# Turning the next expert's gathered rows between the up product and the last expert's down product, with result banks by parity

## What is computed

```python
    combine = jnp.zeros((n, N_EXPERTS), jnp.float32).at[rows[:, None], eid].add(w)
    y = jnp.zeros((n, D_MODEL), jnp.float32)
    for e in range(N_EXPERTS):
        h = jax.nn.silu(xt @ w_gate[e]) * (xt @ w_up[e])
        y = y + combine[:, e:e + 1] * (h @ w_down[e]).astype(jnp.float32)
```

## Time and profile before

| | us |
|---|---|
| median of 3 runs | 955.26 |
| lowest, highest | 954.05, 960.38 |
| the profiled execution | 958.91 |
| span of its profile | 957.2 |
| TensorE busy, products and transposes | 800.9 |
| VectorE, ScalarE, GpSimd busy | 253.7, 172.9, 127.2 |

### The profile page before, as it was taken

One profiled execution on the slowest core, in us unless ns is written; L12 is line 12 of the kernel. 1 busy time (PEld: TensorE's weight loads), 2 busy tenths in 40 slices (PEclk: granted clock), 3 DMA queues, 4 the chain that ended last, 5 costly groups with the idle time before them and its releaser, 6 DMA issues.

```text
span 957.2 us, 14486 instructions
## 1 busy us (share of the span) xinstructions
PE 800.9 (84%) x5352; PEld 576.7 (60%) x5352; DVE 253.7 (27%) x652; ACT 172.9 (18%) x430; POOL 127.2 (13%) x195
## 2 busy tenths in 40 slices
PE   4999999989426856994998579999999999999970
PEld 3474856559305524563454577777777777777740
DVE  2880132020334574663123501110000000000003
ACT  2110111211202612654122110000000000010003
POOL 2103020221431320000000110111111111111010
PEclk9999997989757877997999579999999999999995
DMA  9925341422872843007512537988888888888425
GB/s 375 348 98 169 130 137 49 120 81 80 281 235 61 272 131 140 38 2 302 212 45 74 223 133 265 309 300 307 308 303 303 305 313 301 304 299 314 137 30 205
DMA packets 50201, 192.34 MB, mean 201 GB/s; under 512 B 8129, under 2 KB 25954, under 8 KB 43490
## 3 DMA queue, kind: packets, MB, share of 16 engines
q1 hardware_dynamic: 37346, 155.40, 44.6%
q0 software_dynamic: 12800, 36.22, 13.9%
HBM read 178.20 MB, written 17.33 MB: 204 GB/s over the span
## 4 chain that ended last, share of the span: by engine, by line
PE 72%; issue 9%; DMA 5%; DVE 5%; POOLq 4%; POOL 2%; ACT 2%; SPq 0%; DVEq 0%; ACTq 0%
PE pb L465 66%; POOLq L302 2%; POOL ring L303 2%; PE pb L877 2%; DMA x_rows<-kvn,qbd 1%; PE pb L721 1%; DVE vnr L1673 1%; DMA cst<-in_consts_dram 1%; DMA ring<-in_sel_pages_dram 1%; POOLq L303 1%; PE pb L647 1%; DMA tabs<-in_g_dram 1%; DVE xr L1350 1%; PE pb L790 1%; DVE xr L1391 1%
## 5 line engine op out<-in xcount | busy, mean ns | idle before, releaser
L465 PE MATMUL pb<-vnr,ring 128*128 128x128 f32 x2048 | 235.1, 277 | 12.6 <-DVE vnr L1673 12.6
L465 PEld LDWEIGHTS pb<-vnr,ring 128*128 128x128 f32 x2048 | 232.0, 193 | 16.6 <-DVE vnr L1673 16.6
L465 PE MATMUL pb<-ring,xr 128*32 128x128 f32 (+3 forms) x896 | 143.2, 370 | 0.0
L465 PE MATMUL pb<-ring,qT 128*128 128x512 f32 x256 | 112.6, 592 | 0.9 <-DVE kvn L1688 0.9
L465 PEld LDWEIGHTS pb<-ring,xr 128*32 128x32 f32 (+1 forms) x896 | 74.6, 138 | 62.4 <-issue 59.5
L465 PEld LDWEIGHTS pb<-ring,qT 128*128 128x128 f32 x256 | 47.4, 190 | 55.3 <-issue 55.3
L1678 DVE TENSOR_TENSOR qT<-qT,pb 128x512 f32<-128x512 f32 x16 | 11.0, 688 | 236.5 <-PE pb L465 236.5
L1801 POOL DMA_INDIRECT x_rows<-kvn,qbd x16 | 25.3, 1579 | 330.5 <-DVE kvn L1688 330.5
L465 PE MATMUL pb<-ring 128*128 128x128 f32 (+1 forms) x512 | 63.5, 289 | 4.5 <-DMA ring<-in_cmp_pages_dram 3.3
L465 PEld LDWEIGHTS pb<-ring 128*128 128x128 f32 x512 | 62.7, 201 | 5.1 <-issue 3.7
L465 PE MATMUL pb<-ring,work 128*128 128x512 f32 (+2 forms) x256 | 62.8, 473 | 0.0
(11 more groups left out here) (296 smaller groups left out, 666.1 us busy)
## 6 DMA issues: line engine op xcount, KB each, us to landing
ring<-in_w_gate_dram SPq DMA_DIRECT2D x16, 2048.0 KB, 9.1
ring<-in_w_up_dram SPq DMA_DIRECT2D x16, 2048.0 KB, 8.6
ring<-in_w_down_dram SPq DMA_DIRECT2D x16, 2048.0 KB, 10.1
ring<-in_cmp_pages_dram SPq DMA_DIRECT2D x65, 128.0 KB, 2.8
ring<-in_w_in_dram SPq DMA_DIRECT2D x4, 2048.0 KB, 9.9
ring<-in_sel_pages_dram SPq DMA_DIRECT2D x64, 128.0 KB, 2.9
ring<-in_sel_pages_dram POOLq DMA_DIRECT2D x64, 128.0 KB, 3.0
ring<-in_cmp_pages_dram POOLq DMA_DIRECT2D x63, 128.0 KB, 2.9
```

Source lines behind the costliest of these rows:

```text
L465: return nc.tensor.matmul(out, lhsT, rhs, start=start, stop=stop)
```

## The change

The transposes become a unit of their own, `rows_turned`, which TensorE calls through the new argument `ahead` of `expert_units`. T of n+1 then stands behind U of n and ahead of D of n-1; T0 and T1 stand directly ahead of their G, as before. The result banks of D go by parity: pb4 and pb5 for even experts, pb6 and pb7 for odd ones. The semaphore `y_out` is split in two, one for each scaling engine, and D of n waits for the scalings of n-2. ScalarE now does silu n, copy n+1, scale n-1; VectorE copy n+1, multiply n, scale n-1. TensorE waits for the flag ahead of the experts, since the flag's value was formed in pb7. The part for further passes gets waits of its own and does not run here. SP's order of loads and POOL's order of gathers and adds are as before.

```diff
@@ -269,23 +269,32 @@
             if not isinstance(value, int) or value > 0:
                 eng.wait_ge(sem(name), value)
 
-        def expert_units(b, first, eng, last):
-
-
+        def expert_units(b, first, eng, last, ahead=None):
 
             def unit(e, half, par):
 
                 return e, b * E + e, par, b * (E // 2) + half
 
+            def turn(*u):
+
+                if ahead is not None:
+                    ahead(*unit(*u))
+
+            turn(0, 0, 0)
             first(*unit(0, 0, 0))
+            turn(1, 0, 1)
             first(*unit(1, 0, 1))
+            turn(2, 1, 0)
             last(*unit(0, 0, 0))
             first(*unit(2, 1, 0))
+            turn(3, 1, 1)
             last(*unit(1, 0, 1))
             with eng.Fori(1, E // 2 - 1) as m:
                 first(*unit(2 * m + 1, m, 1))
+                turn(2 * m + 2, m + 1, 0)
                 last(*unit(2 * m, m, 0))
                 first(*unit(2 * m + 2, m + 1, 0))
+                turn(2 * m + 3, m + 1, 1)
                 last(*unit(2 * m + 1, m, 1))
             first(*unit(E - 1, E // 2 - 1, 1))
             last(*unit(E - 2, E // 2 - 1, 0))
@@ -870,13 +879,16 @@
 
             slot_table(0)
 
-            def gate_up(e, n, par, turn):
+            def rows_turned(e, n, par, turn):
+
                 te.wait_ge(sem("xe_in%d" % par), 16 * (turn + 1))
                 after(te, "xt_ready", 2 * n)
                 for k in range(KD):
                     ins = nc.tensor.transpose(pb[k // 4][:, P * (k % 4):P * (k % 4) + CAP],
                                               xe[par][0:CAP, P * k:P * k + P], ident[0:CAP, 0:CAP])
                 ins.then_inc(sem("xt_mm"), 1)
+
+            def gate_up(e, n, par, turn):
                 te.wait_ge(sem("xt_ready"), 2 * n + 2)
                 after(te, "h_ready", n)
                 for slots, bank, weights, done in ((WG, 2, "wg_in", "g_mm"), (WU, 3, "wu_in", "u_mm")):
@@ -891,21 +903,25 @@
             def down(e, n, par, turn):
                 te.wait_ge(sem("h_ready"), n + 1)
                 te.wait_ge(sem("wd_in%d" % par), 16 * (turn + 1))
-                after(te, "y_out", 2 * n)
+                after(te, "y_out0", n - 1)
+                after(te, "y_out1", n - 1)
                 wv = ring[:, WD[par], :].rearrange("p (f n) -> p f n", f=FE)
                 for c in range(2):
                     for f in range(FE):
-                        ins = mm(pb[4 + c][0:CAP, :], he[par][:, f, 0:CAP], wv[:, f, W * c:W * c + W], f == 0, f == FE - 1)
+                        ins = mm(pb[4 + 2 * par + c][0:CAP, :], he[par][:, f, 0:CAP], wv[:, f, W * c:W * c + W], f == 0, f == FE - 1)
                     ins.then_inc(sem("y_mm"), 1)
 
-            expert_units(0, gate_up, te, down)
             te.wait_ge(sem("flag_ready"), 1)
+            expert_units(0, gate_up, te, down, rows_turned)
             more = te.value_load(ints[0:1, 80:81], min_val=0, max_val=1)
             with te.If(more != 0):
+                te.wait_ge(sem("y_out0"), E)
+                te.wait_ge(sem("y_out1"), E)
                 for b in range(1, PASSES):
                     slot_table(b)
+                te.wait_ge(sem("slots_ready"), 2 * PASSES)
                 with te.Fori(1, PASSES) as b:
-                    expert_units(b, gate_up, te, down)
+                    expert_units(b, gate_up, te, down, rows_turned)
 
 
         @block.scalar
@@ -1146,30 +1162,35 @@
             act.wait_ge(sem("rt_shifted"), 2)
             A(rt[:, 260:265], rt[:, 260:265], ACT.Exp).then_inc(sem("rt_exp"), 1)
 
-            def turn_silu(e, n, par, turn):
+            def rows_out(n):
+
+                par = n % 2
                 act.wait_ge(sem("xt_mm"), n + 1)
                 after(act, "u_mm", n - 1)
                 nc.scalar.copy(xeT[par][:, 0:4, 0:CAP], pb[0][:, :].rearrange("p (k n) -> p k n", k=4)[:, :, 0:CAP]
                                ).then_inc(sem("xt_ready"), 1)
+
+            def silu(n):
+
+                par = n % 2
                 act.wait_ge(sem("g_mm"), n + 1)
                 after(act, "h_ready", n - 1)
                 A(sg[par][:, :, 0:CAP], pb[2][:, 0:FE * CAP].rearrange("p (f n) -> p f n", f=FE), ACT.Silu).then_inc(sem("silu"), 1)
 
-            def turned(n):
-
-                turn_silu(n % E, n, n % 2, n // 2)
-
             def y_out(n):
                 act.wait_ge(sem("y_mm"), 2 * n + 1)
                 after(act, "y_added", 16 * (n - 1))
-                A(ye[n % 2][0:CAP, 0:512], pb[4][0:CAP, :], ACT.Copy, scale=slot_w[0:CAP, n:n + 1]).then_inc(sem("y_out"), 1)
+                A(ye[n % 2][0:CAP, 0:512], pb[4 + 2 * (n % 2)][0:CAP, :], ACT.Copy, scale=slot_w[0:CAP, n:n + 1]).then_inc(sem("y_out0"), 1)
 
             def experts(b):
 
-                turned(E * b)
-                for n in range(E * b + 1, E * b + E):
-                    turned(n)
-                    y_out(n - 1)
+                rows_out(E * b)
+                for n in range(E * b, E * b + E):
+                    silu(n)
+                    if n + 1 < E * b + E:
+                        rows_out(n + 1)
+                    if n > E * b:
+                        y_out(n - 1)
                 y_out(E * b + E - 1)
 
             act.wait_ge(sem("slots_ready"), 2)
@@ -1667,33 +1688,38 @@
             V.tensor_copy(ints[:, 80:81], top).then_inc(sem("flag_ready"), 1)
             dve.wait_ge(sem("flag_ready"), 1)
 
-            def turn_mult(e, n, par, turn):
+            def rows_out(n):
+
+                par = n % 2
                 dve.wait_ge(sem("xt_mm"), n + 1)
                 after(dve, "u_mm", n - 1)
                 V.tensor_copy(xeT[par][:, 4:8, 0:CAP], pb[1][:, :].rearrange("p (k n) -> p k n", k=4)[:, :, 0:CAP]
                               ).then_inc(sem("xt_ready"), 1)
+
+            def multiplied(n):
+
+                par = n % 2
                 dve.wait_ge(sem("u_mm"), n + 1)
                 dve.wait_ge(sem("silu"), n + 1)
                 after(dve, "y_mm", 2 * n - 2)
                 V.tensor_tensor(he[par][:, :, 0:CAP], sg[par][:, :, 0:CAP], pb[3][:, 0:FE * CAP].rearrange("p (f n) -> p f n", f=FE), ALU.mult
                                 ).then_inc(sem("h_ready"), 1)
 
-            def turned(n):
-
-                turn_mult(n % E, n, n % 2, n // 2)
-
             def y_out(n):
                 dve.wait_ge(sem("y_mm"), 2 * n + 2)
                 after(dve, "y_added", 16 * (n - 1))
-                V.tensor_scalar(ye[n % 2][0:CAP, 512:1024], pb[5][0:CAP, :], slot_w[0:CAP, n:n + 1], None, ALU.mult
-                                ).then_inc(sem("y_out"), 1)
+                V.tensor_scalar(ye[n % 2][0:CAP, 512:1024], pb[5 + 2 * (n % 2)][0:CAP, :], slot_w[0:CAP, n:n + 1], None, ALU.mult
+                                ).then_inc(sem("y_out1"), 1)
 
             def experts(b):
 
-                turned(E * b)
-                for n in range(E * b + 1, E * b + E):
-                    turned(n)
-                    y_out(n - 1)
+                rows_out(E * b)
+                for n in range(E * b, E * b + E):
+                    if n + 1 < E * b + E:
+                        rows_out(n + 1)
+                    multiplied(n)
+                    if n > E * b:
+                        y_out(n - 1)
                 y_out(E * b + E - 1)
 
             dve.wait_ge(sem("slots_ready"), 2)
@@ -1796,7 +1822,8 @@
 
             def added(n):
 
-                po.wait_ge(sem("y_out"), 2 * n + 2)
+                po.wait_ge(sem("y_out0"), n + 1)
+                po.wait_ge(sem("y_out1"), n + 1)
                 after(po, "y_added", 16 * n)
                 po.indirect_dma_start(scratch_x3, bass.IndirectOffsetOnAxis(slot_tokens[0:CAP, n:n + 1].bitcast(U32), 0),
                                       ye[n % 2][0:CAP, :], None, compute_op=ALU.add).then_inc(sem("y_added"), 16)
```

## The result

The changed kernel takes 965.51 us (median of 11 runs, 955.51 to 971.97), the kernel before 956.07 (11 runs, 954.05 to 960.38). The ratio is 1.0098, 95% interval 1.0065 to 1.0131: 1% slower, where 1.7% faster had been forecast. The profiled execution took 970.78 us, its span is 969.0. Three of the eleven executions, this one among them, lie more than 1.5% above the fastest and are left out of the ratio.

The account below looks back on a forecast made before the run. TensorE alone was taken to bound the expert loop, 23.08 us per expert. Span: 957.2 - 16.1 (stops) - 1.2 (last down products) + 1 (gathers) = 940.9 us; from the median 955.3 - 16.3 = 939.0 us, range 935.5 to 946.5.

Parts of the forecast that it names:

- the stop: TensorE's pause between transposes and first gate product: 1.15 us each, lower bound 0.78; 14 removed, 16.1 us.
- the second loss: Behind the stop, the first gate product is dearer by some 0.2 us; 0.22 counted in each stop.
- The last two down products: Down 15 no longer waits for the scaling of down 14's bank: 1.2 us saved.
- The later multiplication on VectorE: Silu times up comes 1.6 us later, behind the next rows' copy; hidden, with 5 us to spare.
- The split semaphore: Split y_out adds a wait to a down product and POOL's add, on events long past or as late as before.
- The deadline: Transposes of n+2 follow at +13.98 from the end of down n-1, so a gather may take 10.6 us.
- the term of 1 us for the gathers: Loss from late gathers in the loop: 1 us taken, between nothing and about 3.4 us in all.
- the step on the queues: With engines alternating by packet, an earlier gate load waits behind the down load; the gather's share stays, sum 1 us better.
- the signs of being wrong: Gathers over 10.6 us in most experts, a wait for weights, or a loop clock that leaves 1.00.
- The rival of the late gather: Late gathers hold transposes, then down; period 11.35 + L for a gather of L; 946 to 947 us at 11.2; chance 0.14.
- The three cases of late gathers: Gathers late in part, 943 to 949 us, 0.14; nothing gained, 0.05; slower by more than 1%, 0.03.
- the last rival: Slower: adds and gathers queue behind weights to L = 13, period 24.3, 13 of them lose 16 us; about 970; chance 0.03.

Follow-up runs that it names:

- e1_gather_ahead: Changed kernel, with the gather of n+3 ahead of the add of n on POOL's queue, issued one period earlier; 939.64 us, ratio 0.9897.
- e3_banks_only: Changed kernel's banks by parity and split semaphore, with the order of the kernel before; 952.61 us, ratio 0.9981.
- e4_one_wait: Changed kernel, with POOL waiting for one semaphore ahead of an add instead of two; 969.99 us, ratio 1.0165.
- e2_gate_late: Changed kernel, with the gate load issued when the up product has ended instead of the gate product, 7 us later; 937.78 us, ratio 0.9842.
- the second profile: The changed kernel run once more without an edit; 964.19 us, ratio 1.007.
- e9_gate_silu: Changed kernel, with the gate load issued when ScalarE's silu has ended, 0.6 us later; 941.75 us, ratio 0.9869.
- e6_no_add: Changed kernel, with POOL's accumulating add transfers left out; 925.44 us in one run.
- e8_before_down_late: Kernel before, with the down load issued 1.6 us later, behind the next rows' copies; 950.5 us in one run.

## Why the prediction was wrong

**What bounds the kernel, and the stop: right, slightly over-sized.** A stop was put at 1.15 us, between 0.78 and 1.15. The periods measure 23.08 - 22.03 = 1.05. Fourteen of them are 14.7 us, not 16.1. The over-sized part is the second loss: gate and up take 14.29 us by start times in e1_gather_ahead, so they gain 0.10 on the 14.39 and not 0.22.

**The last two down products: right.** 1.2 forecast, 1.35 in e3_banks_only.

**The later multiplication on VectorE: hidden but for one time.** The prediction had 5 us to spare because gate n+1 comes only after a down product. Ahead of gate 1 no down product stands. There TensorE waits for the copy and then the multiplication, which frees the bank of the up product: the 1.4 us of the rows above where 0.78 stood, 0.6 us more.

**The split semaphore "as late as before": wrong in size, free in effect.** It delays the gather's issue by 0.4 to 0.5 us, which e4_one_wait shows not to matter.

These steps give -14.7 - 1.35 + 0.6 = -15.5 us, and e1_gather_ahead's loop is 358.3 - 373.8 = -15.5.

**The gather: the step that failed.** The deadline was right: the transposes start at +13.96 to +14.10 in e1_gather_ahead, +13.98 was worked out, and in the changed kernel they waited for the gathers that landed later than about +14. So was the period with a late gather: 11.35 + 13.3 = 24.65, and the down products of two such experts start 782.30 - 757.48 = 24.8 us apart. What failed is the term of 1 us for the gathers, "a gather gains up to 1 us": the median gained 4.3, from 8.9 to 13.2. With it failed the step on the queues: that the gate load would wait behind a down load "hardly ever" gone, because "down lands after 10.1 us". A landing is not the time in which a load holds the engines. By the packets the down load has mostly passed at +7; the landing only says when the last of it is in. Between +7 and +10 the engines belong to q0, and behind +10 the gate load, issued 2 us earlier, came in with more packets ahead of q0's end. I had priced contention as a share of bandwidth over the overlap (2 us, a third less each). It came as a few small packets that went out late among large ones, and the slowest gather took 14.6 us where the median before was 8.9. Of the signs of being wrong, two came: gathers over 10.6 us in most experts, and a clock in the loop below 1.00.

The Trainium skill (DMA: Bandwidth & Descriptors, "Queues, rings and completion order") has the engines alternate between queues by packet. The trace agrees where both queues are full: in e2_gate_late, from 649.5 to 653.5 us, they moved 64 and 61 packets.

```profile
q1 hardware_dynamic: 64, 1.05, 68.3%
q0 software_dynamic: 61, 0.25, 32.2%
```

It does not bear out what I drew from it, that the gather's time would stay the same. A turn by packet is no equal share when one side's packets are 16 KB and the other's 4 KB or less.

**The second loss, the clock: not in the sum.** The rival of the late gather charged the wait and 0.2 us for the restart. The loop's down products were busy 119.0 - 112.6 = 6.4 us longer and the transposes 18.1 - 15.6 = 2.5 (lines of 560 to 940 us). With the waits of 21.9 and nine restarts of 0.2, the prediction's estimate, that makes 32.6; against e1_gather_ahead the loop is 391.1 - 358.3 = 32.8 us longer. Most of the longer work is the clock: the five stretches at 0.50 are some 17 us together, and half of that is 8.5. So a microsecond of waiting cost one and a half here. In the second profile 16.2 us of waits cost 25.6, with four such stretches; in e4_one_wait 21.1 cost 28.8, with three. The two profiles of the changed kernel are of executions 5 to 6 us above their medians; by the medians it loses 965.5 - 939.6 = 26 us to e1_gather_ahead.

**The chances.** The right rival was there, with its place and its formula, and the row that spoke for it: 0.2 us of slack in the slowest gathers. The three cases of late gathers got 0.22 together, and slower by more than 1% got 0.03; the range left out some 0.15 above. That the last rival's 970 lies close to the 965.5 is in part luck: it had all 13 gathers late and nothing for the clock, and nine were late and the clock made up for the other four.

What stays open: why so small a shift, 0.6 us of the gate load's issue, decides it, what holds q0 back until about +6, and on which of the 16 engines the last packets wait. The rows by queue don't tell the engines apart. The theory that the gate load's distance decides rests on e9_gate_silu and e2_gate_late, with e6_no_add for the add's part; I have no run that makes the kernel before slow in this way, and e8_before_down_late, meant to, did not.

Each of e1_gather_ahead, e2_gate_late and e9_gate_silu is faster than both kernels, by 1.0 to 1.6% over the one before, and they can't be told apart by their intervals. e1_gather_ahead needs no timing to fall right, since its gathers are issued a period earlier.

## What to carry to other kernels

When a consumer moves ahead of the work that used to cover its transfer, move the transfer's issue by as much; the distance from issue to need should exceed the longest transfer seen by more than a small part of it. The latencies of the old order hold only for its own order of transfers: ask which load's issue moves against which, and look at packets by queue, microsecond by microsecond, since landings don't show who held the engines. And a wait that TensorE takes in the middle of dense work can cost half as much again, most of it through the clock (1.4 to 1.6 times in three profiles here).

## What the hardware showed that I had not expected

A gather of at most 128 rows of 4 KB took 4.3 to 5.1 us ahead of the loop (the first three of the kernel before) and 8.9 in the loop; it rose to a median of 12.7 in e1_gather_ahead, where the 2 MB loads (gate behind down, up behind gate, down behind up) were issued 7.3, 7.0 and 7.9 us apart instead of 9.2, 7.0 and 7.0, and fell to 8.4 in e9_gate_silu with 7.9, 6.4 and 7.9. In the slow case 22 small packets took six microseconds.

After 3.9 us of rest and about half a microsecond of work the granted clock was 0.50 for about 3 us, and the down product took 8.04 us in place of 6.88.
